# Feed-forward in two phases, one output tile at a time, with lead and rest halves side by side

## What is computed

```python
for i in range(2):
    h = h + 0.5 * swiglu(rms_norm_2(h, ffn1_norm[i]), ffn1_w_gate[i], ffn1_w_up[i], ffn1_w_down[i])
    hn = rms_norm_2(h, mix_norm[i])
    m = rglru_mixer(hn, ...) if i == 0 else pool_mixer(hn, ...)
    h = h + m
    h = h + 0.5 * swiglu(rms_norm_2(h, ffn2_norm[i]), ffn2_w_gate[i], ffn2_w_up[i], ffn2_w_down[i])
    gate = jax.nn.sigmoid(rms_norm_2(h, ple_norm[i]) @ ple_w_gate[i])
    h = h + gate * (p[i] @ ple_w_proj[i])
return rms_norm_2(h, final_norm)

def swiglu(x, w_gate, w_up, w_down):
    return (jax.nn.silu(x @ w_gate) * (x @ w_up)) @ w_down
```

## Time and profile before

| | us |
|---|---|
| median of 3 runs | 2600.95 (2598.21 to 2602.36) |
| the profiled execution, device time | 2601.42 |
| its span, from first to last instruction | 2599.6 |
| mean granted TensorE clock | 0.985 |
| first block, up to the first product of ffn 0 | 1564.3 |
| PE busy, DVE busy, ACT busy | 2354.7, 1058.2, 800.8 |

### The profile page before, as it was taken

How to read it: one execution, slowest core, us unless ns; L and a number is a source line. 1 busy time by engine, 2 the same in 40 slices (tenths; PEclk the granted TensorE clock), 3 DMA queues, 4 the chain that set the end, 5 groups by cost and what they waited for, 6 DMA issues and landing times.

```text
span 2599.6 us, 32943 instructions
## 1 busy us (share of the span) xinstructions
PE 2354.7 (91%) x14544; PEld 1646.4 (63%) x14566; DVE 1058.2 (41%) x1407; ACT 800.8 (31%) x983; POOL 67.6 (3%) x99
## 2 busy tenths in 40 slices
PE   6998899888887997998887879999999999989997
PEld 3855653433332675632222229998899989979997
DVE  5536441111010665401000116557755565565555
ACT  4425421010100545210000015434644354424433
POOL 0023000000000021000000000000000000010000
PEclk9998899999999998899999999999999999999999
DMA  6292268999999340399999994544444445443441
GB/s 276 114 393 121 98 259 366 428 427 429 427 429 427 119 168 1 133 425 428 428 428 428 428 429 146 188 173 156 169 172 171 157 170 194 168 156 115 176 178 69
DMA packets 49865, 660.57 MB, mean 254 GB/s; under 512 B 5616, under 2 KB 7152, under 8 KB 8144
## 3 DMA queue, kind: packets, MB, share of 16 engines
q1 hardware_dynamic: 48640, 653.67, 61.8%
q0 software_dynamic: 1104, 5.11, 0.5%
HBM read 657.71 MB, written 1.05 MB: 253 GB/s over the span
## 4 chain that ended last, share of the span: by engine, by line
PE 61%; DMA 26%; DVE 7%; ACT 5%; issue 1%; SPq 0%; POOL 0%; DVEq 0%; ACTq 0%; POOLq 0%
DMA ring<-in_exp_up 17%; PE ps L678 13%; PE ps L679 13%; PE ps L680 13%; PE ps L1043 7%; DMA ring<-in_exp_down 6%; PE ps L1067 3%; DMA ring<-in_ada_w 2%; PE ps L551 2%; DVE ring_r L367 1%; PE ps L832 1%; ACT ring_r L360 1%; PE ps L716 1%; PE ps L1163 1%; PE ps L855 1%
## 5 line engine op out<-in xcount | busy, mean ns | idle before, releaser
L1043 PE MATMUL ps<-ring,arena 128*64 128x512 f32 (+1 forms) x2048 | 460.4, 597 | 96.0 <-DMA ring<-in_exp_up 53.7
L678 PE MATMUL ps<-h_buf_r,ring_r 128*128 128x256 f32 (+1 forms) x1856 | 538.0, 290 | 9.4 <-DVE arena_r L1906 5.2
L680 PE MATMUL ps<-h_buf_r,ring_r 128*128 128x256 f32 (+1 forms) x1856 | 535.0, 288 | 0.0
L367 DVE TENSOR_TENSOR ring_r<-ring,ring_r 128x4096 fp32r<-128x4096 f32 (+2 forms) x97 | 406.1, 4192 | 284.1 <-ACT ring_r L360 284.1
L679 PE MATMUL ps<-h_buf_r,ring_r 128*128 128x256 f32 x1696 | 479.9, 283 | 0.0
L360 ACT ACTIVATE ring_r<-ring 128x4096 fp32r<-128x4096 f32 (+2 forms) x97 | 332.7, 3434 | 245.0 <-DMA ring<-in_ffn_w 218.7
L1043 PEld LDWEIGHTS ps<-ring,arena 128*64 128x64 f32 (+1 forms) x2048 | 128.6, 123 | 423.6 <-issue 268.7
L678 PEld LDWEIGHTS ps<-h_buf_r,ring_r 128*128 128x128 f32 x1856 | 356.9, 192 | 16.7 <-issue 9.5
L680 PEld LDWEIGHTS ps<-h_buf_r,ring_r 128*128 128x128 f32 x1856 | 357.0, 192 | 3.3
L679 PEld LDWEIGHTS ps<-h_buf_r,ring_r 128*128 128x128 f32 x1696 | 325.5, 192 | 0.2
L679 PE MATMUL ps<-arena_r,ring_r 128*128 128x256 f32 (+1 forms) x944 | 277.2, 294 | 0.0
(11 more groups left out here) (273 smaller groups left out, 2569.0 us busy)
## 6 DMA issues: line engine op xcount, KB each, us to landing
ring<-in_exp_gate SPq DMA_DIRECT2D x64, 2048.0 KB, 25.4
ring<-in_exp_up SPq DMA_DIRECT2D x64, 2048.0 KB, 25.6
ring<-in_exp_down SPq DMA_DIRECT2D x64, 2048.0 KB, 23.7
ring<-in_ffn_w SPq DMA_DIRECT2D x60, 2048.0 KB, 7.7
ring<-in_ada_w SPq DMA_DIRECT2D x24, 2048.0 KB, 17.2
ring<-in_w_in SPq DMA_DIRECT2D x6, 2048.0 KB, 15.6
ring<-in_ffn_w SPq DMA_DIRECT2D x12, 1024.0 KB, 4.8
ring<-in_lru_w SPq DMA_DIRECT2D x6, 2048.0 KB, 8.0
```

Source lines behind the costliest of these rows:

```text
L367: dve.tensor_tensor(rest, slot(n)[:, 0:halved[n]], lead, ALU.subtract).then_inc(sem("chunk_halved"), 1)
L678: release(pe.matmul(out, a[0], b[0], start=start, stop=False, skip_group_check=True))
L680: return pe.matmul(out, a[1], b[0], start=False, stop=stop, skip_group_check=True)
L1043: mm = pe.matmul(ps[half * m:half * m + m, which, :], xe[:, k, :], slot(c)[:, at:at + 512], start=k == 0, stop=k == KT - 1)
```

## The change

A feed-forward now has two phases. In the first, eleven chunks each hold two gate tiles and two up tiles with all eight input tiles. In the second, eight chunks each hold all 22 inner tiles of the weight for one output tile. Leads and rests of an activation lie side by side, and a new `wide` makes a product of two matmuls: the weight's lead by 512 columns (lead and rest), then the weight's rest by the 256 columns of the lead. The halves of the bank are added on the way out: ACT copies the columns 256 to 511, DVE adds the columns 0 to 255 to the copy.

When an output tile is finished, it is added to the residual, and its square, lead and rest for the next stage are made at once, while PE makes the next tile. The first chunk of a feed-forward goes input tile by input tile over four banks. Squares are summed on DVE (`add_square`), and PE makes two matmuls of a norm's sum where it made eight (`norm_mean`). The recurrent mixer's output product also goes output tile by output tile. In the last stage of a layer (`ple`) the product with `p` comes ahead of the gate product and is copied out of PSUM. The output is stored in two parts. In the diff below, `wide` and the first `ffn` are PE's, `ffn_evict` and the second `ffn` are DVE's (ACT's runs in the same order), and the last two pieces are PE's in the recurrent mixer and in `ple`.

```diff
+            def wide(bank, w, lo, both, start, stop):
+                release(pe.matmul(ps[:, bank, :], w[0][:, lo:lo + P], both, start=start, stop=False, skip_group_check=True))
+                return pe.matmul(ps[:, bank, 0:N], w[1][:, lo:lo + P], both[:, 0:N], start=False, stop=stop, skip_group_check=True)
...
             def ffn(i, norm):
                 n = chunk_at["ffn", i]
-                open_sums()
-                with pe.Fori(0, FT // 8) as it:
-                    ffn_group(i, norm, n, it, 0, 4)
-                    ffn_group(i, norm, n + 3, it, 4, 4)
...
+                for c in range(PAIRED):
+                    w, banks = halves(n + c), gate_banks(c) + up_banks(c)
+                    if c == 0:
+                        for k in range(KT):
+                            if k in (0, KT // 2):
+                                halved_chunk(n, min(k, parts_of[n] - 1))
+                            norm_tile(pe, norm, k)
+                            for t in range(4):
+                                mm = wide(banks[t], w, 4 * P * k + P * t, h_buf_r[:, k, :], k == 0, k == KT - 1)
...
+                    else:
+                        halved_chunk(n + c)
+                        for t in range(4):
+                            if c >= 2 and t % 2 == 0:
+                                pe.wait_ge(sem(("ffn_gate_read", "ffn_up_read")[t // 2]), PAIRED * i + c - 1)
...
+                    if c == 0:
+                        norm_mean(pe, release, norm)
+                for d in range(KT):
+                    halved_chunk(n + PAIRED + d)
...
+                    for f in range(FT):
+                        if d == 0 and f % 2 == 0:
+                            pe.wait_ge(sem("ffn_halved"), PAIRED * i + f // 2 + 1)
+                        mm = wide(d, w, P * f, hid[:, f, :], f == 0, f == FT - 1)
+                    mm.then_inc(sem("ffn_summed"), 1)
...
+            def ffn_evict(i, c):
+                dve.wait_ge(sem("ffn_gate_rest"), done + 1)
+                dve.tensor_tensor(gates, ps[:, bank:bank + 2, 0:N], gates, ALU.add)\
+                    .then_inc(sem("ffn_gate_read"), 1)
+                dve.tensor_tensor(gates, gates, bc_mid(rstd2, 2), ALU.mult).then_inc(sem("ffn_gate_scaled"), 1)
+                dve.tensor_tensor(hidden, ps[:, up:up + 2, 0:N], hidden, ALU.add)\
+                    .then_inc(sem("ffn_up_read"), 1)
+                dve.tensor_tensor(hidden, gates, hidden, ALU.mult).then_inc(sem("ffn_hid"), 1)
+                dve.tensor_tensor(hid[:, 2 * c:2 * c + 2, N:2 * N], hidden, hid[:, 2 * c:2 * c + 2, 0:N], ALU.subtract)\
+                    .then_inc(sem("ffn_halved"), 1)
...
             def ffn(i, norm, gain, following):
+                for c in range(1, PAIRED):
+                    ffn_evict(i, c - 1)
+                    halve_rest(dve, chunks[c + 2])
+                ffn_evict(i, PAIRED - 1)
+                for d in range(KT):
+                    if d:
+                        ffn_add(i, d - 1)
+                        next_tile(norm + 1, d - 1, gain)
+                    if PAIRED + d + 2 < len(chunks) and d < KT - 1:
+                        halve_rest(dve, chunks[PAIRED + d + 2])
+                ffn_add(i, KT - 1)
+                next_tile(norm + 1, KT - 1, gain)
+                if len(following) > 1:
+                    halve_rest(dve, following[1])
...
                 for k in range(RT):
+                        if d == 0:
+                            pe.wait_ge(sem("lru_y"), k + 1)
...
+                pe.wait_ge(sem("ple_proj_copied"), 4 * l + 2)
+                norm_mean(pe, release, norm)
```

More of the change, by code:

```diff
@@ L44 @@
 CONV = 4
+PLE_TILES = ((6, 7), (0, 2), (2, 4), (4, 6), (7, 8))
+PLE_ORDER = (6, 0, 1, 2, 3, 4, 5, 7)
 POOLS = (2, 4, 8, 16)
@@ L326, in build @@
             stream(("ffn", 2 * l + 1), *FFN_CHUNKS)
-            stream(("ple", l), HALVED, (2, 2 * D + 2 * N), HALVED)
+            stream(("ple", l), (1, 2 * D + 2 * N), HALVED, HALVED)
+        parts_of = [2 if n == chunk_at["ffn", 0] else 1 for n in range(len(loads))]
         slot_of, rest_of = [], []
@@ L1663, in _ @@
-            norm_squares(act, LAST_NORM, ("ple_added", KT * (LAYERS - 1), 1))
+                if l == 0:
+                    halve_lead(act, chunk_at["w_in", 1])
+            n, gain, start = chunk_at["ffn", 0], norm_gain("ffn1_norm", 0), LAST_GROUP + before("moe_added", 1)
+            halve_lead(act, n, 0)
+            for d in range(KT):
+                act.wait_ge(sem("moe_added"), start + d + 1)
+                lead(act, d, gain)
+                if d == 1:
+                    halve_lead(act, n, 1)
@@ new lines, in _ @@
+            for d in range(KT):
+                square(act, 2 * LAYERS, d)
+            halve_lead(act, n + 1)
+            f = [chunk_at["ffn", i] for i in range(2 * LAYERS)]
+            ffn(0, 4, norm_gain("mix_norm", 0), (chunk_at["lru", 0], chunk_at["lru", 0] + 1))
+            lru()
+            ffn(1, 6, norm_gain("ple_norm", 0), (chunk_at["ple", 0], chunk_at["ple", 0] + 1))
+            ple(0, 7, norm_gain("ffn1_norm", 1), (f[2], f[2] + 1))
+            ffn(2, 8, None, ())
+            pooling()
@@ L1664, in _ @@
+            ffn(3, 10, norm_gain("ple_norm", 1), (chunk_at["ple", 1], chunk_at["ple", 1] + 1))
+            ple(1, 11, None, ())
             norm_act(act, LAST_NORM, rstd2)
@@ L2196, in pooling, with ple @@
                     dve.tensor_tensor(x, x, pool_y[:, d, :], ALU.add).then_inc(sem("pool_added"), 1)
-            def ple(l):
+                    if d:
+                        rest(dve, POOL_NORM + 1, d - 1, following)
+                rest(dve, POOL_NORM + 1, KT - 1, following)
+                for d in range(KT):
+                    add_square(dve, POOL_NORM + 1, d)
+                halve_rest(dve, chunk_at["ffn", 3] + 1)
+            def ple(l, norm, gain, following):
                 n = chunk_at["ple", l]
-                halve_rest(dve, n + 1)
+                factors(norm)
@@ new lines, in ple @@
+                scaled(1)
+                scaled(2)
+                add(1)
+                scaled(3)
+                add(2)
+                add(3)
+                for j in range(1, 7):
+                    add_square(dve, norm + 1, j, PLE_ORDER)
+                scaled(4)
+                if gain:
+                    rest(dve, norm + 1, 0, gain)
+                add(4)
+                if gain:
+                    for d in range(1, KT):
+                        rest(dve, norm + 1, d, gain)
```

658 lines of the change are left out of this document (354 added, 304 removed).

## The result

The changed kernel takes 2571.8 us (median, 2568.9 to 2574.3); the kernel before, run beside it, 2599.8. The ratio is 0.9891, 95% interval 0.9879 to 0.9903. So it is 28 us faster where 15 were forecast.

The account below looks back on a forecast made before the run. PE's matmul count and start distance were taken to bound the feed-forwards. Stage terms of -27 us plus 12 us for the clock gave -15 from 2601.4 us, so 2586 us as median, range 2567 to 2605.

Parts of the forecast that it names:

- Part 1: Feed-forward products: the wide matmul makes each 0.3467 us instead of 0.360, 28.1 us less over four feed-forwards.
- the turn: First phase: one round of eviction and halving between DVE and ACT per chunk, 11.6 us against PE's 11.1.
- Part 2: Feed-forward eviction and halving: may replace PE as bound, costing PE 1 to 4 us per feed-forward plus one 3.8 us wait.
- The wait for the last hidden pair: First output tile of a feed-forward's second phase: PE waits 3.8 us, in each of four feed-forwards.
- Part 3: Stage exits and entries, tile by tile: ffn 0 entry 5.0 us earlier, pooling -12.0, but waits at second chunks.
- The mixer: Recurrent mixer's output, tile by tile: about 4.5 us lost at its head, won back at its end; entered as 0.
- I take seven, 12 us: Clock falls at PE's waits, 1.7 us each: bounds none, 0 us, and thirteen, 22 us; seven taken, 12 us.
- The sum without the clock: All stages from the entry of ffn 0 to the final norm, before the clock charge: together -27 us.
- B: Rival: the clock stays up and the chain keeps pace, 2568 to 2575 us; chance 0.18.
- C: Rival: clock falls at every wait and longer handovers, about 2599 us, no change; chance 0.13.
- D: Rival: slower, the turn between ACT and DVE lengthened by handovers of 0.16 us, paid 44 times, 2626 us; chance 0.10.
- E: Rival: the pair of 512 and 256 columns costs 0.360 us like three matmuls, 2596 us, no change; chance 0.05.

Follow-up runs that it names:

- e4_fill: Changed kernel plus matmuls of zeros put where PE waits, to hold the clock up; 2562.7 us, ratio 0.9861 to the kernel before.
- the reordered kernel: Changed kernel with halvings moved: on ACT directly behind silu, on DVE directly behind the hidden product; 2554.4 us, ratio 0.9836; repeat 2557.8 us, 0.9832.

## Why the prediction was right or wrong

**Part 1** had the pace right (0.3475 for 0.3467 us) and also said that its 28 us would not all arrive. With the turn as it is, 5 us arrive. They are there only after the halvings are moved. The rule of the Trainium skill (page "TensorE: Matmul & The Clock Gate", section "Wait — 56ns, not 53.3ns?"), 2.5 ns per matmul, is not what this format shows: 512 columns take 0.23 us to the next start and 256 take 0.12, and undoing the merge with PE as the bound cost 23 us by the blocks, 10.7 ns a product, where 2.5 ns would make 5. The matmuls of zeros in `e4_fill`, 512 columns in bf16, do start 0.216 us apart, as that rule has it; so what it misses here is the format.

**Part 2** named the right bound and the right chain. The turn was put at 11.6 and is 11.43: I had added printed lengths and a handover, but an instruction's successor starts up to 0.09 us before its printed end (4.43 printed, 4.34 to the next start). The wait for the last hidden pair was put at 3.8 us, four times, 15.2 in all; measured 9.2. The turn is shorter, so the chain is less late when the phase ends; the 4.1 to 4.5 us with a turn of 12.03 fit that.

**Part 3** put the entry of ffn 0 right to a tenth, the entry of ffn 2 at 4.6 (4.1 measured), `ple` at 3.0 and 2.4 (1.5 and 2.4), and the second chunks of ffn 0, 1 and 3 at 10.8 us together, where 1.34, 2.27 and 3.23 were measured; why these are shorter is open. Pooling brought 9.7 where 12.0 were due. The mixer was put at 0 and became 3.6 us shorter. I had reckoned 4.5 us lost at its head and 7 won back at its end, and yet entered nothing; no run takes its tile-by-tile output apart.

**The step that failed** is the last one, "I take seven, 12 us" for the clock, laid in full on top of waits that the sum had already charged in full. The sum without the clock, -26.9, is all but what was measured with it, -28.1. Two terms were too large. The clock falls: there were seven more places than before (nine stretches of 3.4 us), but removing eight stretches brought 8.0 us, 1.0 us each and not 1.7. The waits: 16.0 us were measured where the sum had 26.0 (6.0 less at the hidden pairs, 4.0 less at the second chunks). With the mixer's 3.6 us and some 4 at the clock that makes about 18 us on one side; ffn 2 and pooling, together 4.9 us worse than forecast, take part of it back. That the two charges were made for the same gap, each as if the other were not there, fits `e4_fill`, whose gain before the last hidden pair is next to nothing; it is argued, not shown. The forecast of the median, 2586, is 14 us too high; 2571.8 lies inside the range of 2567 to 2605. That the part without the clock comes so near is in part luck, as its waits were too long and its pooling and ffn 2 too good.

**The rivals.** B had the time (2568 to 2575) and the wrong reason. C is out, since its 22 us for the clock are not there. D's mechanism is real: its price of 44 times what is added to the turn was measured, 27.0 us for 44 x 0.60. Its condition, longer handovers, did not come true. E's condition, a pair as slow as three matmuls, is false. Its reckoning, with PE at 11.5 us a chunk and the turn nearly equal, is the picture of the kernels with three matmuls.

## What to carry to other kernels

When two engines hand work to each other in lists of fixed order, add up one whole turn of that exchange from starts, and compare it with the bound engine's time for the same piece; busy shares of 44% and 33% of the span, and still of 70% and 49% within the phase, hid a turn that set the pace, and PE's 100% hid that it would have to wait at the end. If the two are within a few per cent, a gain on one side shows only once the other has moved too, so try the edits together and apart before either is judged. Where a long operation may stand before a short one that waits, put it into the wait: moving the two halvings ahead of their waits brought 21 us, four times what the merged matmul had brought beside the old turn.

## What the runs showed of the hardware that I had not expected

**A clock fall far from the change comes in some executions and not in others.** In the first block, whose code is the same, the granted clock is at half for 10.2 us in some executions and not in others. The kernel before and then the changed one, same place:

```profile
1091.60:1101.80 10.20, 9.37 (x38) 6.35 (x39) 1.73 (x5) 0.60 (x1) 0.00 (x0) 0.52 0.01 2
```

```profile
1091.40:1101.60 10.20, 9.37 (x57) 5.03 (x58) 2.01 (x6) 0.60 (x1) 0.00 (x0) 1.00 0.20 48
```

PE starts 38 matmuls there instead of 57. Both kinds occur with one and the same kernel: the reordered kernel had the fall in its first profile and not in its second, and its last scatter began at 1555.5 and at 1550.7. In all, its first block was at half clock for 64.9 and 54.6 us. That difference is as large as half of the effects studied here, and it is why the length of the second block was the better measure.

**Operations on both halves of a PSUM bank cost what the nearest rows said.** An ACT copy of two banks' second halves takes 0.58 us and a DVE sum of their first halves 0.68, against 0.69 for a DVE operation of the same size outside PSUM.
